# MLA and grouped-query attention: the ninth probability tile of a unit is transposed behind the other eight, into a bank of the next score set, and copied out by ScalarE

## What is computed

```python
def mha_blocks(q, k, v):
    scale = q.shape[-1] ** -0.5
    def blk(qb):
        s = jnp.einsum('bqhd,bkhd->bhqk', qb, k).astype(jnp.float32) * scale
        p = jax.nn.softmax(s, axis=-1).astype(v.dtype)
        return jnp.einsum('bhqk,bkhd->bqhd', p, v)
    return over_query_blocks(blk, q)
```

## Time and profile before

| | |
|---|---|
| median of 3 runs | 2457.29 us (2454.61 to 2463.05) |
| span of the profiled execution, first to last instruction | 2454.1 us |
| profiled span against the median | 3.2 us less |
| TensorE products, weight loads | 93%, 65% of the span |
| VectorE, ScalarE, GpSimd | 54%, 37%, 10% |
| mean granted TensorE clock | 0.984 of full |

### The profile page before, as it was taken

The page is one execution under the profiler, slowest core; times in us unless marked ns, Lnnn a source line. Parts: engine busy times, 40 slices in busy tenths (PEclk is TensorE's granted clock), DMA queues, the critical chain, the costliest instruction groups (busy, mean ns, idle before and its releaser), DMA issues. The chain is left out here.

```text
span 2454.1 us, 36381 instructions
## 1 busy us (share of the span) xinstructions
PE 2283.0 (93%) x14536; PEld 1589.0 (65%) x14536; DVE 1337.4 (54%) x2554; ACT 916.4 (37%) x1824; POOL 254.3 (10%) x400
## 2 busy tenths in 40 slices
PE   6999999899999998989989999999999999889898
PEld 3656865685466776764856577657844667768657
DVE  3642764564646466583546337555645664755832
ACT  2332113452245256383224221135521542744821
POOL 0310001000100011021314000010011000110213
PEclk9999999899999999999999999999999999999999
DMA  8710100100020000113265101001001100001022
GB/s 280 269 36 29 56 18 1 53 2 15 1 77 2 4 4 7 36 36 130 77 232 202 48 16 56 18 3 52 1 15 37 41 2 5 3 7 54 18 86 86
DMA packets 75151, 129.64 MB, mean 53 GB/s; under 512 B 25794, under 2 KB 38978, under 8 KB 73348
## 3 DMA queue, kind: packets, MB, share of 16 engines
q1 hardware_dynamic: 73960, 121.65, 14.4%
q10 hardware_dynamic: 1024, 5.67, 0.7%
HBM read 110.10 MB, written 21.92 MB: 54 GB/s over the span
## 5 line engine op out<-in xcount | busy, mean ns | idle before, releaser
L659 PE MATMUL psum<-arena 128*32 128x128 f32 (+9 forms) x9392 | 1504.0, 391 | 65.4 <-issue 11.9
L659 PEld LDWEIGHTS psum<-arena 128*32 128x32 f32 (+3 forms) x9392 | 927.1, 150 | 569.1 <-issue 419.4
L663 PE MATMUL psum<-ident,arena 128*128 128x128 f32 (+1 forms) x2248 | 351.9, 281 | 78.3 <-ACT arena L1542 34.5
L1721 DVE TENSOR_TENSOR arena<-arena 128x256 f32<-128x256 f32 (+10 forms) x710 | 318.9, 494 | 146.6 <-ACT arena L1416 42.6
L663 PEld LDWEIGHTS psum<-ident,arena 128*128 128x128 f32 (+1 forms) x2248 | 252.7, 141 | 182.7 <-issue 115.0
L659 PE MATMUL psum<-k_parts,q_parts 96*128 96x384 f32 (+2 forms) x1000 | 284.2, 373 | 16.0 <-ACT arena L1451 4.7
L1721 DVE TENSOR_TENSOR arena<-psum,arena 128x512 f32<-128x512 f32 (+2 forms) x116 | 68.2, 596 | 257.2 <-PE psum L659 254.9
L2018 DVE TENSOR_REDUCE st<-psum 128x1 f32<-128x1152 f32 (+1 forms) x144 | 178.0, 1237 | 48.7 <-PE psum L659 48.4
L2113 DVE TENSOR_REDUCE st<-psum 128x1 f32<-128x1152 f32 (+1 forms) x144 | 174.2, 1236 | 52.0 <-PE psum L659 51.7
L659 PEld LDWEIGHTS psum<-k_parts,q_parts 96*128 96x128 f32 (+1 forms) x1000 | 170.7, 195 | 33.0 <-issue 16.7
L1451 ACT ACTIVATE arena<-psum,st 128x1152 f32<-128x1152 f32 (+1 forms) x144 | 162.4, 1128 | 76.0 <-DVE st L2018 73.4
(11 more groups left out here) (146 smaller groups left out, 1649.1 us busy)
## 6 DMA issues: line engine op xcount, KB each, us to landing
arena<-in_ada_w SPq DMA_DIRECT2D x12, 2048.0 KB, 8.3
arena<-in_w_in SPq DMA_DIRECT2D x10, 2048.0 KB, 8.0
arena<-out_xs SPq DMA_DIRECT2D x36, 512.0 KB, 5.6
out_xs<-arena SPq DMA_DIRECT2D x18, 512.0 KB, 2.6
arena<-in_w_out SPq DMA_DIRECT2D x4, 2048.0 KB, 8.0
out_xs<-in_x ACTq DMA_DIRECT2D x1, 4608.0 KB, 19.3
spectrum_kept<-arena SPq DMA_DIRECT2D x2, 2304.0 KB, 8.7
arena<-spectrum_kept SPq DMA_DIRECT2D x2, 2304.0 KB, 8.8
```

What stands on the lines that cost most here:

```text
L659: return nc.tensor.matmul(out, lhsT, rhs, start=start, stop=stop)
L663: return nc.tensor.transpose(out, src, ident[0:n, 0:n])
L1721: return nc.vector.tensor_tensor(out, a, b, op)
```

## The change

Of a unit that is not late, the ninth tile (piece 2) is transposed in the same step as the other eight, behind them. It goes into the third bank of the score set that the next step writes (bank 2 or 5), and ScalarE copies it, between piece 0 and the step's exponential. TensorE waits for the exponential of the unit ahead, which read that bank, before the tile, and for ScalarE's copy before the third score chunk of the next step. Late units keep their banks, engines and order. Of 32 units with three pieces 25 are not late, in each of two attentions and two layers.

```diff
 def piece_engine(grp, u, j):
-    return ("scalar", "vector", "vector")[j]
+    return ("scalar", "vector", "vector" if due(grp, u + 2) else "scalar")[j]
...
 def turn_bank(grp, u, j):
-    return (6, 7, 6)[j] if due(grp, u + 2) else (7, 6, 7)[j]
+    return (6, 7, 6)[j] if due(grp, u + 2) else (7, 6, 3 * ((u + 3) % 2) + 2)[j]
...
                             out, ks = bank[3 * (x % 2) + j][:, 0:w], slice(c, c + w)
+                            if 3 * (x % 2) + j in side:
+                                pe.wait_ge(*side.pop(3 * (x % 2) + j))
...
                         b, buf = turn_bank(grp, u, j), PROB[grp] + (u % 3) * 1152
+                        if b < 6 and u + 1 < len(units):
+                            pe.wait_ge(*S.at("exps", (grp, u + 1)))
                         take_bank(b, S.at(turned_by[number], (grp, number)))
...
                         for c in (0, 1, 2):
                             if new:
                                 scores(g, c)
-                            if last_turn and c == 0:
-                                turn(g - 3, 1 if behind else 2)
-                            if last_turn and behind and c == 1:
-                                turn(g - 3, 2)
+                            if last_turn and behind and c < 2:
+                                turn(g - 3, 1 + c)
...
                         if old and not late(grp, g):
                             turn(g - 2, 1)
+                            turn(g - 2, 2)
...
                     for g in range(tail_step(grp)):
-                        if late(grp, g - 1):
-                            take(g - 3, 1)
-                        take(g - 3, 2)
                         if not late(grp, g):
                             take(g - 2, 0)
+                            take(g - 2, 2)
                         if g < len(units):
                             exps(g)
...
                         if late(grp, g - 1):
                             take(g - 3, 1)
-                        take(g - 3, 2)
+                            take(g - 3, 2)
```

## The result

| | before | after |
|---|---|---|
| median of the runs | 2455.95 us (2450.69 to 2463.05, 4 runs) | 2435.71 us (2435.3 to 2437.75, 4 runs) |
| span of the profiled execution | 2454.1 us | 2434.2 us (its own time 2435.95) |

The ratio is 0.9917 [0.9903, 0.9932]: the changed kernel is faster by 20 us, where 14 were forecast (2443.0, range 2435 to 2452; the median lies 0.7 us inside its lower end). Two repeats gave a smaller gain, 0.9938 [0.9919, 0.9957] and 0.9942 [0.9918, 0.9965], 16 and 14 us; 14 to 20 us is what can be said of it.

The account below looks back on a forecast made before the run. TensorE, busy 93% of the span, was taken as the bound. Per layer MLA 0.8 + 1.4 and GQA 3.6 + 1.2 make 7.0 us, 14.0 for both: 2454.1 - 14.0 + 3.2 gives 2443, range 2435 to 2452.

Parts of the forecast that it names:

- The ninth tile in its row: TensorE's transposes: a ninth tile behind the other eight costs 0.10 us; nothing saved by this in MLA.
- The third chunk's wait for the ninth's copy: Next step's third score chunk: wait taken as 0; other end 0.15 us for each of 50 GQA steps, 7 us.
- The last cycles: Last cycle of each attention stretch, where short prompt scores hide nothing: 1.2 us less in GQA, 1.4 in MLA.
- No TensorE wait on L2032 in the last cycles: Sign for the forecast: in each stretch's last cycle TensorE no longer waits on that line.
- the cycle of 13.7 us: Sign for the forecast: GQA cycles, from value burst to value burst, take 13.7 instead of 14.2 us.
- Copy by ScalarE: Ninth copies move from VectorE to ScalarE: its GQA step becomes 2.15 us, above TensorE's 2.07; MLA has room.
- The loop through maximum and exponential: GQA products, VectorE's maximum, ScalarE's exponential and ninth tile, over two steps: 4.3 us, or 2.15 a step.
- MLA cycle: MLA, burst to burst: 0.08 us wait for VectorE's ninth copy goes, plus 0.03 for three tiles: 0.11 us.
- B: Rival, chance 0.13: shorter waits also keep the granted clock up in layer 1's last cycles; 2439 us.
- A: The main forecast, chance 0.60: gains as laid out for GQA, MLA and last cycles; 2443 us, 2438 to 2448.
- C: Rival, chance 0.22: ScalarE paces GQA steps, 0.2 us longer than laid out; regular GQA cycles gain nothing; 2450.5 us.
- D: Rival, chance 0.05: slower, as GQA waits drop the clock mid-stretch, 6 us a cycle; 2467 us with four.

Follow-up runs that it names:

- e8: Kernel after, with one more ScalarE copy of 96 columns, used by nothing, behind each ninth tile's copy; 2435.27 us, 0.9912.
- e9: Kernel after, with ScalarE instead of VectorE copying the late unit's second four tiles; 2438.23 us, 0.9929.
- e12: Kernel after, late unit's second four copied by ScalarE, its pieces in spare bank, 6, 7; other units' first and second four in 6, 7; 2423.12 us, 0.9878.
- e1: Kernel before, run again with no edit; 2456.65 us, 0.9998.
- e3: Kernel after, with the change in GQA alone and MLA in the old order; 2443.7 us, 0.9943.
- e5: Kernel before, with only the ninth copies moved to ScalarE, old place and bank kept; 2495.07 us, 1.0159.
- e4: Kernel after, with the change in MLA alone and GQA in the old order; 2450.69 us, 0.9988.
- e11: Kernel after, run again with no edit, the second repeat; 2439.66 us, 0.9942.

## Why the prediction was right, and where it was not

**What held.** The ninth tile in its row costs a tenth of a us: nine tiles take 0.90, 0.10 each. The Trainium skill, "TensorE: Matmul & The Clock Gate", section "Back-to-back issue gap", has 81 ns; the rows went against it here again. TensorE's own GQA step was forecast as 2.07 and is 2.03 to 2.07. The third chunk's wait for the ninth's copy costs nothing behind ScalarE: six products take 1.13 to 1.14 us (739.06 to 740.20), with 1.15 due. The last cycles gave 1.19 and 1.39 in GQA against 1.2, and 1.40 in MLA against 1.4. What is late next is the exponential ahead of the ninth tile, 0.17 us, though in one GQA step of a cycle and not in each. Two of the signs need a word. "No TensorE wait on L2032 in the last cycles" contradicts the working, which kept one such wait of 0.7 us, and it is there, 0.66 [<-DVE L2033]. And the cycle of 13.7 us was met by luck: the 14.2 that it started from is found only in the second cycle of a stretch (14.23); the steady ones took 14.40, and 14.40 - 0.5 is 13.9.

**Step *Copy by ScalarE*: 2.15 us mis-sized, about 1.92 measured.** I added durations and a gap, 0.59 + 0.27 + 0.08. ScalarE's next instruction starts before the last has ended, and 0.71 passes from the first copy's start to the exponential's, which makes 1.92 with the 1.21. The loop through maximum and exponential, forecast as 4.3 for two steps, took 743.21 - 739.03 = 4.18 from one ninth tile to the next but one, 2.09 a step. TensorE's own 2.07 and 2.03 therefore set the pace of two steps, and only in the third does the exponential come late. A steady GQA cycle gains 0.72 instead of the 0.52 laid out, and the first ones of the stretches 0.84 and 0.97: over both layers 10.2 us instead of 7.2, 3.0 more. e8 shows how far ScalarE is from the pace: 0.51 us of its time a cycle cost 0.09. The late unit's step was taken for unchanged, and the two waits in it stayed as they were; e9 to e12 show that they could go.

**Step *MLA cycle*: 0.11 forecast, 0.01 to 0.02 measured.** I put the 0.08 us ahead of the burst down to VectorE's ninth copy, as the trace names it. With that copy gone the burst still starts 0.27 us behind. It is not that wait, nor is it VectorE's four-tile copy, which had ended 0.51 us before the burst; what it is stays open; the switch to another product is one candidate and was not tried. In MLA's steady cycles 0.2 us came instead of 1.6, 1.4 less. The 0.03 for each tile didn't show either.

**The rivals.** *B, the clock, came true beside A.* MLA's last burst of layer 1 ran at the lower level in all four profiles with the old place of the ninth tile (before, e1, e3 and e5, 5.66 to 5.78 us), and in none of ten with the new. GQA's did in two of four (before, e1; not in e4 and e5), and in none of ten with the new. Between the two profiles of the bill that is 1.7 and 2.7 us. The Trainium skill's Part 1 of the same page, that activity releases the throttled level, agrees with that in direction. I had given it 0.13 for layer 0 keeping its level with the same waits. It does so in before, e1 and e3, but not in e5, whose waits are longer: there MLA's last burst of layer 0 fell too.

```profile
586.51 5.68 PE L659 MATMUL psum<-arena 128*32 128x256 f32 x72 [0.46 <-ACT arena L1466]
```

Why layer 1 loses the level by waits with which layer 0 keeps it stays open. It wasn't tried. Nor do the medians show B's gain by itself: the repeats, with all last bursts at full pace, gained 16 and 14 us; the mean granted clock of their runs lies between 0.980 and 0.985, so it falls elsewhere, and not equally in each run. *C fell*: ScalarE's own step is not 0.2 us longer but 0.2 shorter than laid out, and even doubling the copy gave no C. *D fell*: steady cycles stand at 1.00.

**The sum.** 14.0 forecast; 3.0 more for GQA's cycles, 1.4 less for MLA's, 0.2 more for the last cycles: 15.8, which is what the bill has by the edit. The clock adds 4.1 between the two spans, net: B's 4.4, and falls in other places, which nearly cancel. The forecast also took 3.2 us from the span to the median; the profiled run of the kernel after has 1.75 (2434.2 to 2435.95), and the rest of the 3.2 was spread of the runs. So of the 7.3 us between 2443 and 2435.7 the edit has 1.8, this term 1.4 and the clock 4.1, and the range held by 0.7 us.

## What to carry to other kernels

A small piece that waits in a busy engine's queue may have to change its place in the order, its bank and its copying engine together; with the bank or the engine left as it was, or the engine changed alone, 29 to 39 us were lost here. Lay out an engine's loop by the distances from start to start in the trace, not by a sum of durations. Then look for the step that kept the old order: a GQA cycle gained 0.7 us by the change, and another 0.4 when the late unit followed.

## What the runs showed of the hardware

ScalarE overlaps its instructions: two copies of 0.59 and 0.27 us and the start of an exponential take 0.71 us from start to start, and a further copy of 0.28 us adds 0.17. The same first 27 products of MLA in layer 1 take 6.3 or 9.06 us in executions of one and the same kernel (after and its second repeat, e11), the granted clock being at its upper or its lower level. In layer 0 the lower level stands in both profiles of the kernel before and the upper in all three of the kernel after, but not so in the variants. The windows of layer 0 (0.50 in the kernel before from 456 to 466, 0.52 in e1):

```profile
456.00:466.00 10.00, 9.53 (x30) 9.04 (x31) 3.27 (x4) 3.53 (x5) 0.00 (x0) 0.52 0.00 0
```

That is e1, first score products of layer 0; the kernel after in its own window, by the same columns:

```profile
454.00:466.00 12.00, 9.96 (x62) 9.60 (x63) 7.29 (x7) 7.47 (x12) 0.00 (x0) 1.00 0.01 1
```

The one has 30 instructions in 9.53 busy us, the other 62 in 9.96, some of them transposes. From one score product to the next it is 0.32 us at the lower level and 0.17 to 0.18 at the upper.

That MLA's last cycle of layer 1 loses the upper level under the old order in four profiles of four, and that of layer 0, with the same waits, in none of three, was also new, and is unexplained.
